# Gate and up projections of a feed-forward layer by seven block products instead of eight, and the split of the hidden values moved to the start of the down projection

## The chip, the cores and the metric

The kernel runs on 1 core of one Trainium2 chip. The metric is the device time in microseconds (us); smaller is better. TensorE multiplies, VectorE (DVE), ScalarE (ACT) and GpSimd (POOL) do elementwise work, SyncE (SP) issues the weight transfers.

## The reference, cut to what matters

Two transformer blocks over 512 tokens (528 with 16 meta tokens in front in part of the first block), d_model 1024, all in f32. Each block has two feed-forward layers (four in all) around a mixer:

```
h = h + 0.5 * rmsnorm(swiglu(rmsnorm(h, g), w_in, w_out), g2)      # block 1, twice; block 2 without the outer norm
swiglu(x) = (silu(x @ w_gate) * (x @ w_up)) @ w_down                # 1024 -> 2816 twice, 2816 -> 1024
```

D_FF is 2816, that is 22 tiles of 128 columns. The mixers between the feed-forward layers (an mLSTM, and a mixer of attention and retention) are not touched.

## The kernel before, in words

**Precision.** Every f32 operand of a large product is split in two f32r numbers, hi and lo = x - hi, and a product is three matmuls: hi*hi, hi*lo, lo*hi (`product`, L1467; its matmuls stand at L1472). ACT makes hi by a copy, DVE or POOL makes lo by a subtraction. Activations are kept transposed: 8 tiles of 128 features by 512 (or 528) tokens.

**Weights.** They come in units of 128 x 1024 (512 KB) through four slots: SP loads a unit into `raw`, ACT copies it to `whi` (`split_hi`, L454, L468), POOL subtracts into `wlo` (`pool_lo`, L367, L371), PE uses both. The semaphores count units: `raw_loaded`, `hi_done`, `lo_done`, `unit_done`. POOL serves the units strictly in order; ACT works three units ahead (AHEAD = 3). SP loads a unit when the lo of the unit four before is made.

**A feed-forward layer** (`pe_ffn` L1534, `act_ffn` L503, `dve_ffn` L919, `load_ffn` L311) has an up stage and a down stage. Up: for each of 22 tiles two units, gate and up, of 8 k-tiles each, so 48 matmuls of 512 columns (with 528 tokens: 96 of 264 columns, in two pieces). PE waits for `lo_done` of the unit and for the banks. DVE multiplies the gate sums by the norm factors `rbc` (L926), ACT applies silu (L509), DVE multiplies by the up sums (L931) and by rbc (L934), ACT makes hid_hi (L511) and DVE hid_lo (L936), all during the next tile's matmuls. Down: for each of 8 output tiles three units (8, 8 and 6 k-tiles) over the 22 hidden tiles. The first output tile waits, k by k, for `hid_ready`, and each output tile waits for `out_s["v_ready"]`, whose first two counts come from `free_out` (L944), three memsets that DVE issues ahead of `dve_ffn`.

**The norm.** The x operands xhi and xlo are made from hT times the gains before the norm factors are known; the first two tiles of PE's work run while the sum of squares is formed. `r_ready` on DVE waits for rbc, and then `dve_ffn` starts.

The order on each engine is written out by hand: each engine runs its own program in order, and only semaphores tie them together. ACT's and POOL's programs (`prog_scalar`, `prog_gpsimd` L429) call the parts in turn.

## Time and profile before

| what | us |
|---|---|
| median of 3 runs | 2214.21 (2208.22 to 2214.69) |
| the profiled execution's own time | 2211.47 |
| its span, first to last instruction | 2209.7 |
| TensorE busy | 2128.5 (96% of the span) |
| VectorE / ScalarE / GpSimd busy | 744.6 / 719.5 / 925.0 |
| mean granted TensorE clock | 0.98 of full speed |

How to read it: busy time is the union of an engine's instructions; weight loads (PEld) run beside matmuls. A matmul's own duration (some 0.40 us at 512 columns) holds its way through the array; what counts is the distance of one start to the next, which a row of many matmuls gives as its time divided by their number. In rows of the timeline the columns are start, duration, engine, line, operation, output <- inputs, count, and in brackets the idle time before and what ended it.

### The profile page before, as it was taken

The numbers are of one execution on the slowest core, as the hardware profiler recorded it, in microseconds if no ns is written. First come the engines' busy times: TensorE is split into PE (matmuls) and PEld (weight loads), VectorE is DVE, ScalarE is ACT, GpSimd is POOL, SyncE is SP. The second block draws the span as 40 slices with busy tenths as digits, with TensorE's granted clock in tenths as the row PEclk, the third lists the DMA queues.
The fourth block names the chain that finished last, engine by engine and source line by source line (L and its number), as shares of the span: only waits on it lengthen the run. The fifth ranks groups of instructions, "written<-read, shape, count | busy, mean of one in ns | idle before, by whom it ended". The sixth has DMA issues, their size and how long they took to land.

```text
span 2209.7 us, 28883 instructions
## 1 busy us (share of the span) xinstructions
PE 2128.5 (96%) x10959; PEld 1745.8 (79%) x10959; DVE 744.6 (34%) x1084; ACT 719.5 (33%) x993; POOL 925.0 (42%) x402
## 2 busy tenths in 40 slices
PE   8999999899999899999989999999989899999998
PEld 7999999887777688888868888886774377888887
DVE  5222210483374622220062222116657623222111
ACT  4222222333443422222242222224255424222222
POOL 3444344434453544445554444443333033444442
PEclk9999999999899999999999999999999999999999
DMA  5332233223202233323323333333211022333331
GB/s 148 96 95 86 83 94 91 57 65 86 72 1 67 65 97 95 95 88 89 99 67 95 95 95 88 93 96 89 74 39 29 1 67 85 95 95 95 89 95 55
DMA packets 333835, 176.98 MB, mean 80 GB/s; under 512 B 9539, under 2 KB 329278, under 8 KB 333774
## 3 DMA queue, kind: packets, MB, share of 16 engines
q1 hardware_dynamic: 331792, 175.07, 27.2%
q10 hardware_dynamic: 1982, 1.07, 0.2%
q8 instruction: 41, 0.67, 0.1%
q14 instruction: 20, 0.16, 0.0%
HBM read 174.02 MB, written 2.10 MB: 80 GB/s over the span
## 4 chain that ended last, share of the span: by engine, by line
PE 89%; DVE 7%; ACT 2%; issue 1%; DMA 0%; POOL 0%; SPq 0%; ACTq 0%; DVEq 0%; POOLq 0%
PE ps L1472 82%; PE ps L1948 1%; DVE wa L998 1%; DVE E L1023 1%; PE ps L1709 1%; PE ps L1500 1%; PE ps L1914 1%; DVE xlo L891 1%; PE ps L1705 1%; DVE small L1352 0%; DMA x_tok<-in_x 0%; PE ps L1740 0%; PE ps L1924 0%; DVE sinr L1160 0%; ACT PR L735 0%
## 5 line engine op out<-in xcount | busy, mean ns | idle before, releaser
L371 POOL TENSOR_TENSOR wlo<-raw,whi 128x1024 fp32r<-128x1024 f32 x336 | 829.6, 2471 | 1144.6 <-ACT whi L468 1144.4
L1472 PE MATMUL ps<-xhi,whi 128*128 128x512 f32 (+2 forms) x2224 | 728.2, 359 | 28.0 <-DVE xlo L891 17.7
L1472 PE MATMUL ps<-xlo,whi 128*128 128x512 f32 (+2 forms) x2224 | 720.7, 355 | 0.0
L1472 PE MATMUL ps<-xhi,wlo 128*128 128x512 f32 (+2 forms) x2224 | 719.2, 354 | 0.0
L468 ACT ACTIVATE whi<-raw 128x1024 fp32r<-128x1024 f32 x336 | 353.1, 1053 | 515.6 <-PE ps L1472 506.8
L1472 PEld LDWEIGHTS ps<-xhi,whi 128*128 128x128 f32 (+1 forms) x2224 | 392.3, 189 | 101.3 <-issue 21.3
L1472 PEld LDWEIGHTS ps<-xlo,whi 128*128 128x128 f32 (+1 forms) x2224 | 393.8, 190 | 63.6 <-issue 2.0
L1472 PEld LDWEIGHTS ps<-xhi,wlo 128*128 128x128 f32 (+1 forms) x2224 | 393.0, 189 | 61.5
L1472 PE MATMUL ps<-hid_hi,wlo 128*128 128x512 f32 (+1 forms) x880 | 280.5, 351 | 0.0
L1472 PE MATMUL ps<-hid_hi,whi 128*128 128x512 f32 (+1 forms) x880 | 279.5, 350 | 0.0
L1472 PE MATMUL ps<-hid_lo,whi 128*128 128x512 f32 (+1 forms) x880 | 278.9, 350 | 0.0
L511 ACT ACTIVATE hid_hi<-wb 128x512 f32 (+3 forms) x88 | 56.0, 637 | 462.7 <-DVE wb L934 462.7
L931 DVE TENSOR_TENSOR wb<-wa,ps 128x512 f32<-128x512 f32 (+1 forms) x88 | 60.9, 693 | 399.4 <-PE ps L1472 387.7
L1472 PEld LDWEIGHTS ps<-hid_lo,whi 128*128 128x128 f32 x880 | 153.8, 188 | 24.7
L1472 PEld LDWEIGHTS ps<-hid_hi,wlo 128*128 128x128 f32 x880 | 153.6, 188 | 23.5
L1472 PEld LDWEIGHTS ps<-hid_hi,whi 128*128 128x128 f32 x880 | 153.4, 188 | 22.9
L926 DVE TENSOR_TENSOR wa<-ps,rbc 128x512 f32<-128x512 f32 (+1 forms) x88 | 61.2, 695 | 223.3 <-PE ps L1472 206.5
L936 DVE TENSOR_TENSOR hid_lo<-wb,hid_hi 128x512 f32 (+1 forms) x88 | 65.2, 740 | 82.5 <-ACT hid_hi L511 82.5
L969 DVE SCALAR_TENSOR_TENSOR hT<-ps,hT 128x512 f32 x24 | 16.6, 692 | 224.3 <-PE ps L1472 224.3
L965 DVE TENSOR_SCALAR ybuf<-ps,vec 128x528 f32 (+1 forms) x16 | 12.2, 760 | 226.1 <-ACT sq L537 226.1
L934 DVE TENSOR_TENSOR wb<-wb,rbc 128x512 f32<-128x512 f32 (+1 forms) x88 | 62.1, 706 | 3.0
L509 ACT ACTIVATE wa<-wa 128x512 f32<-128x512 f32 (+1 forms) x88 | 54.4, 618 | 1.8 <-DVE wa L926 1.8
...
## 6 DMA issues: line engine op xcount, KB each, us to landing
...
```

The source lines that it names most:

```text
L371: pool.tensor_tensor(wlo[:, u % SLOTS, :], raw[:, u % SLOTS, :], whi[:, u % SLOTS, :].bitcast(F32), ALU.subtract).then_inc(lo_done, 1)
L468: act.activation(whi[:, s, :], raw[:, s, :], ACT.Copy).then_inc(hi_done, 1)
L509: act.activation(tile(wa, b, n), tile(wa, b, n), ACT.Silu).then_inc(s["silu_done"], 1)
L511: act.activation(tile(hid_hi, r * 2 + b, n), tile(wb, b, n), ACT.Copy).then_inc(s["hi_ready"], 1)
L891: v.scalar_tensor_tensor(out=tile(xlo, k, n), in0=tile(hT, k, n), scalar=gain(name, g0 + k), in1=tile(xhi, k, n).bitcast(F32), op0=ALU.mul ...
L926: v.tensor_tensor(tile(wa, b, n), bank(2 * b if n == TOK else b, n), tile(rbc, 0, n), ALU.mult) \
L931: v.tensor_tensor(tile(wb, b, n), tile(wa, b, n), bank(4 + 2 * b if n == TOK else 2 + b, n), ALU.mult) \
L934: v.tensor_tensor(tile(wb, b, n), tile(wb, b, n), tile(rbc, 0, n), ALU.mult).then_inc(s["product"], 1)
L936: v.tensor_tensor(tile(hid_lo, r * 2 + b, n), tile(wb, b, n), tile(hid_hi, r * 2 + b, n).bitcast(F32), ALU.subtract).then_inc(s["hid_ready ...
L998: v.tensor_tensor(tile(wa, k % 2, n), tile(value, k, n), tile(rbc, 0, n), ALU.mult).then_inc(s["t_ready"], 1)
L1023: link(v, "dve", v.scalar_tensor_tensor(out=cacc(b), in0=zpad(b)[:, j:j + TOK], scalar=w[j], in1=cacc(b), op0=ALU.mult, op1=ALU.add))
L1472: ins = pe.matmul(o, lhs[l], x[r], start=first and n == 0, stop=last and n == 2)
```

## The change

In each feed-forward layer 4 of the 22 up tiles (tiles 18 to 21, now first in time; called old tiles below) are made as before. The other 18 are made by Winograd's form of the 2x2 block product: the weights of a tile are four blocks of 512 columns (gate, k-tiles 0-3 = A11; gate, 4-7 = A12; up, 0-3 = A21; up, 4-7 = A22), x is cut in k halves and in token halves. Seven products of 4 k-tiles x 3 matmuls x half the tokens (256 or 264 columns) replace eight.

- Once per layer: DVE makes eight half tiles times gains and rbc twice over (`scaled`, 16 operations of 256 or 264 columns), four `differences` of 1024 (1056) columns; ACT makes seven hi operands of that width, DVE four lo, POOL three. They stand between the four old tiles.
- Per fast tile: ACT copies A21 to a PSUM bank, makes seven hi halves of 512, keeps three partial sums, and applies silu; DVE makes four weight sums, three lo, the corner, gate and hidden operations; POOL makes four lo. Multiplication by rbc after the matmuls is gone.
- The hidden tiles are stored in f32. Their split in hid_hi and hid_lo is made from the last fast tile on and in the first output tile of the down stage, in a new order of k (8..15, 18..21, 16, 17, 0..7). `free_out` is issued by DVE behind `dve_ffn`, ahead of its last ten splits.

The core of the diff (semaphore tables, tile addressing helpers and parts that repeat are left out):

```diff
+    def pool_ffn(pool, i):
+        f, s, n = FFNS[i], fast_s, FFNS[i]["n"]
+        u0 = f["u0"]
+        pool_lo(pool, u0 + AHEAD, u0 + 6)
+        pool.wait_ge(ffn_s["x_diff"], ffn_at[i]["x_diff"] + 4)
+        for q, name in enumerate(("A11", "A12", "S4")):
+            pool.wait_ge(ffn_s["x_hi"], ffn_at[i]["x_hi"] + q + 1)
+            pool.tensor_tensor(x_operand(xop, name, 1, n), x_operand(xop_f, name, 1, n),
+                               x_operand(xop, name, 0, n).bitcast(F32), ALU.subtract).then_inc(ffn_s["x_lo_pool"], 1)
+        pool_lo(pool, u0 + 6, u0 + 2 * NCONV)
...
+        def body(st):
+            r, c = st
+            nxt = (r, c + 1)
+            lo(st, "S3", operand(stage, i, "S3"), s["w_lo_pool"], 1)
+            more = r is not None or c + 1 < NFAST
+            if more:
+                lo(nxt, "A11", raw_blocks(i, c + 1)["A11"], s["w_lo_pool"], 1)
+                lo(st, "A22", raw_blocks(i, c)["A22"], s["w_lo_pool"], 1)
+                lo(nxt, "A12", raw_blocks(i, c + 1)["A12"], s["w_lo_pool"], 1)
+            else:
...
+        def hid_hi(first, last):
+            for at_ in range(first, last):
+                k = HID_ORDER[at_]
+                act.wait_ge(c_s["hid"], hid_made(i, k))
+                act.wait_ge(*freed_by(i, at_ ))
+                act.activation(hid_hi_tile(k, n), hid_tile(k, n), ACT.Copy).then_inc(c_s["hid_hi"], 1)
...
+        def body(st):
+            r, c = st
+            nxt = (r, c + 1)
+            first, last = r is None and c == 0, r is None and c == NFAST - 1
+            a, b, d = acc_banks(c)
...
+            keep(st, "M1", kept(n)[:, 0, :], a, free)
+            hi_sum(st, "S3", "M7")
+            if not last:
+                keep_a21(nxt)
+                hi_a11(nxt)
+            else:
+                hid_hi(0, 4)
+            keep(st, "M5", m5_of(n), d, None if first else done(i, "c22", before(st)))
+            if not last:
+                hi_sum(nxt, "S1", "M5")
+            else:
+                down_hi(0)
+            hi(st, "A22", raw_blocks(i, c)["A22"], "M4")
+            if last:
+                hid_hi(4, 7)
+            keep(st, "M6", kept(n)[:, 1, :], a, None)
+            if not last:
+                hi_sum(nxt, "S2", "M6")
+                hi(nxt, "A12", raw_blocks(i, c + 1)["A12"], "M2")
+            else:
+                hid_hi(7, 10)
+                down_hi(1)
+            act.wait_ge(*done(i, "gate", st))
+            act.activation(gates_of(n), gates_of(n), ACT.Silu).then_inc(s["silu"], 1)
+        split_to_conv(act, u0, 1)
+        silu(0)
+        split_to_conv(act, u0, 3)
+        x_hi(("A11", "A12", "S4"), c_s["x_ready"], c_at["x_ready"] + 1)
+        silu(1)
+        split_to_conv(act, u0, 5)
+        x_hi(("S1", "S3", "S2", "A22"), c_s["x_diff"], c_at["x_diff"])
+        silu(2)
...
+        if n == SEQ:
+            prepare()
+        silu(3)
+        if n == TOK:
...
+    def dve_ffn(v, i, rms, name, g0):
...
+        def conv(q):
+            b = q % 2
+            v.wait_ge(unit_done, STARTED + u0 + 2 * q + 1)
+            v.wait_ge(c_s["banks_free"], c_at["banks_free"] + q + 1)
+            v.tensor_tensor(tile(wa, b, n), bank(2 * b if n == TOK else b, n), tile(rbc, 0, n), ALU.mult) \
+             .then_inc(c_s["gate_scaled"], 1)
...
+            v.wait_ge(unit_done, STARTED + u0 + 2 * q + 2)
+            if q >= 2:
+                v.wait_ge(c_s["hid"], c_at["hid"] + q - 1)
+            v.tensor_tensor(tile(wb, b, n), tile(wa, b, n), bank(4 + 2 * b if n == TOK else 2 + b, n), ALU.mult) \
+             .then_inc(c_s["banks_free"], 1)
+            v.wait_ge(c_s["banks_free"], c_at["banks_free"] + q + 3)
+            v.tensor_tensor(tile(hid_f, NFAST + q, n), tile(wb, b, n), tile(rbc, 0, n), ALU.mult).then_inc(c_s["hid"], 1)
...
+        def scaled():
...
+            for g, ks in enumerate(((0, 1, 2, 3), (4, 5, 6, 7))):
+                for half in range(2):
+                    for k in ks:
+                        span = slice(o + half * h, o + (half + 1) * h)
...
+                    ins.then_inc(c_s["x_ready"], 1)
...
+        def differences():
+            part = lambda name: x_operand(xop_f, name, 1, n)
+            b12 = hid_f[:, B12_AT * TOK:B12_AT * TOK + 4 * h]
+            v.wait_ge(c_s["x_ready"], c_at["x_ready"] + 4)
+            v.tensor_tensor(part("S1"), b12, part("A11"), ALU.subtract).then_inc(c_s["x_diff"], 1)
+            v.tensor_tensor(part("S3"), part("S4"), b12, ALU.subtract).then_inc(c_s["x_diff"], 1)
+            v.wait_ge(c_s["x_diff"], c_at["x_diff"] + 1)
+            v.tensor_tensor(part("S2"), part("S4"), part("S1"), ALU.subtract).then_inc(c_s["x_diff"], 1)
+            v.wait_ge(c_s["x_diff"], c_at["x_diff"] + 3)
+            v.tensor_tensor(part("A22"), part("A12"), part("S2"), ALU.subtract).then_inc(c_s["x_diff"], 1)
+        def x_lo():
+            v.wait_ge(c_s["x_diff"], c_at["x_diff"] + 4)
+            for q, name in enumerate(("S1", "S3", "S2", "A22")):
+                v.wait_ge(c_s["x_hi"], c_at["x_hi"] + 4 + q)
+                v.tensor_tensor(x_operand(xop, name, 1, n), x_operand(xop_f, name, 1, n),
+                                x_operand(xop, name, 0, n).bitcast(F32), ALU.subtract).then_inc(c_s["x_lo_dve"], 1)
...
+        def corner(st):
+            a = acc_banks(st[1])[0]
+            v.wait_ge(*done(i, "M7", st))
+            v.wait_ge(*done(i, "m5_kept", st))
+            r, c = st
+            if not (r is None and c == 0):
+                v.wait_ge(c_s["hid"], count(c_at["hid"] + NCONV, st))
+            v.tensor_tensor(c22_of(n), ps[:, a, 0:h], m5_of(n), ALU.add).then_inc(s["c22"], 1)
...
+        def hidden(st):
+            r, c = st
+            a = acc_banks(c)[0]
+            if r is None and c == NFAST - 1:
+                v.wait_ge(unit_done, STARTED + u0 + NU_UP)
+            else:
+                v.wait_ge(*done(i, "M4", st))
+            v.wait_ge(*done(i, "silu", st))
+            v.wait_ge(*done(i, "c22", st))
+            v.tensor_tensor(hid_half(st, 0, n), ps[:, a, 0:h], gates_of(n)[:, 0, :], ALU.mult)
+            v.tensor_tensor(hid_half(st, 1, n), c22_of(n), gates_of(n)[:, 1, :], ALU.mult).then_inc(c_s["hid"], 1)
+        def hid_lo(first, last):
+            for at_ in range(first, last):
+                k = HID_ORDER[at_]
+                v.wait_ge(c_s["hid_hi"], c_at["hid_hi"] + at_ + 1)
+                if k < HID_IN_XLO:
+                    v.wait_ge(*freed_by(i, KF + k))
+                v.tensor_tensor(hid_lo_tile(k, n), hid_tile(k, n), hid_hi_tile(k, n).bitcast(F32), ALU.subtract) \
+                 .then_inc(c_s["hid_ready"], 1)
+        def body(st):
+            r, c = st
+            nxt, prev = (r, c + 1), (r, c - 1)
+            first, last = r is None and c == 0, r is None and c == NFAST - 1
+            if not first:
+                corner(prev)
+            lo(st, "S2")
+            s3(st)
+            lo(st, "S4")
+            if not last:
+                s1(nxt)
+                lo(nxt, "S1")
+            else:
+                hid_lo(0, 4)
+            if not first:
+                hidden(prev)
+            if not last:
+                s2(nxt)
+            else:
+                hid_lo(4, 8)
+            gate(st)
+            if not last:
+                s4(nxt)
+        conv(0)
+        scaled()
+        conv(1)
+        differences()
+        conv(2)
+        x_lo()
+        start = (None, 0)
+        if n == SEQ:
+            s1(start)
+            lo(start, "S1")
+            s2(start)
+        conv(3)
+        if n == TOK:
+            s1(start)
+            lo(start, "S1")
+            s2(start)
+        s4(start)
+        body(start)
+        with v.Fori(0, NFAST // 2 - 1) as r:
+            body((r, 1))
+            body((r, 2))
+        end = (None, NFAST - 1)
+        body(end)
+        corner(end)
+        hid_lo(8, 10)
+        hidden(end)
+        hid_lo(10, 12)
+        v.wait_ge(c_s["hid"], c_at["hid"] + KF)
+        def rest():
+            hid_lo(12, KF)
+        return rest
...
         free_out(v, 2, SEQ)
-        dve_ffn(v, 1, N2)
+        rest()
...
+        for q in range(2, NCONV):
+            for g in range(2):
+                unit(q // 2, q % 2, g)
+        pe_fast(pe, i)
...
                     pe.wait_ge(lo_done, r * 12 + (u + 1))
-                    for k in range(k0, k0 + kn):
+                    for k in piece:
                         if j == 0:
-                            pe.wait_ge(s["hid_ready"], at["hid_ready"] + k + 3)
-                        ins = product(pe, [o for o, _, _ in p], w_tile(u, k - k0),
...
+    def pe_fast(pe, i):
...
+        def multiply(name, bank_, start):
+            w = [operand(buf, i, name) for buf in (whi, wlo)]
+            x = [x_operand(xop, name, low, n) for low in range(2)]
+            for k in range(4):
+                for q, (l, r) in enumerate(((0, 0), (0, 1), (1, 0))):
+                    ins = pe.matmul(ps[:, bank_, 0:h], w[l][:, k * P:(k + 1) * P], x[r][:, k * h:(k + 1) * h],
+                                    start=start and k == 0 and q == 0, stop=k == 3 and q == 2, skip_group_check=True)
+            return ins
...
+        def body(st):
+            r, c = st
+            a, b, d = acc_banks(c)
+            first = r is None and c == 0
+            pe.wait_ge(*done(i, "lo_A11", st))
+            if first:
+                pe.wait_ge(c_s["banks_free"], c_at["banks_free"] + NCONV + 1)
+                pe.wait_ge(c_s["x_lo_pool"], c_at["x_lo_pool"] + 1)
+            elif r is None:
...
+            pe.wait_ge(*done(i, "lo_S1", st))
+            if first:
+                pe.wait_ge(c_s["gate_scaled"], c_at["gate_scaled"] + NCONV)
+                pe.wait_ge(c_s["x_lo_dve"], c_at["x_lo_dve"] + 4)
+                pe.wait_ge(c_s["x_lo_pool"], c_at["x_lo_pool"] + 3)
+            multiply("S1", d, True).then_inc(s["mult"], 2 if first else 1)
+            if not first:
+                m4((r, c - 1))
+            pe.wait_ge(*done(i, "lo_S2", st))
+            pe.wait_ge(*done(i, "m1_kept", st))
+            multiply("S2", a, False).then_inc(s["mult"], 1)
+            pe.wait_ge(*done(i, "lo_A12", st))
+            multiply("A12", b, True).then_inc(s["mult"], 1)
+            pe.wait_ge(*done(i, "lo_S4", st))
+            pe.wait_ge(*done(i, "m5_kept", st))
+            multiply("S4", d, False).then_inc(s["mult"], 1)
+            pe.wait_ge(*done(i, "lo_S3", st))
+            pe.wait_ge(*done(i, "u2_kept", st))
+            multiply("S3", a, False).then_inc(s["mult"], 1)
+        body((None, 0))
+        with pe.Fori(0, NFAST // 2 - 1) as r:
+            body((r, 1))
+            body((r, 2))
+        end = (None, NFAST - 1)
+        body(end)
+        m4(end)
```

## Rows read from the trace of the kernel before

**Rows 1.** The page: engines' busy time, and the chain that ended last by engine.
```profile
PE 2128.5 (96%) x10959; PEld 1745.8 (79%) x10959; DVE 744.6 (34%) x1084; ACT 719.5 (33%) x993; POOL 925.0 (42%) x402
...
PE 89%; DVE 7%; ACT 2%; issue 1%; DMA 0%; POOL 0%; SPq 0%; ACTq 0%; DVEq 0%; POOLq 0%
```

**Rows 2.** The chain in order of time, pieces of matmuls: start us, us, what.
```profile
39.78 370.07 PE ps L1472 x3042
...
1134.23 1.78 PE ps L1500 x16
...
1138.64 355.53 PE ps L1472 x1530
```

**Rows 3.** Windows of 512-column and of 264-column matmuls: stretch, us, busy by engine, clock.
```profile
59.50:71.20 11.70, 11.70 (x98) 11.70 (x98) 2.83 (x4) 3.20 (x4) 4.79 (x2) 1.00 0.32 93
1863.00:1874.15 11.15, 11.15 (x50) 9.02 (x49) 2.77 (x4) 3.17 (x4) 4.82 (x2) 1.00 0.32 94
```

**Rows 4.** Groups on VectorE: name, shapes, count | busy us, mean ns | idle.
```profile
L1088 DVE SCALAR_TENSOR_TENSOR E<-ps,E 128x512 f32<-128x512 f32 x8 | 5.5, 692 | 0.4
...
L1088 DVE SCALAR_TENSOR_TENSOR E<-ps,E 128x256 f32<-128x256 f32 x8 | 3.4, 425 | 0.3
```

**Rows 5.** Groups on ScalarE: copies of 1024 and 512, activations of 256.
```profile
L468 ACT ACTIVATE whi<-raw 128x1024 fp32r<-128x1024 f32 x336 | 353.1, 1053 | 515.6 <-PE ps L1472 506.8 <-DMA raw<-in_ffn_w_in 5.6 <-issue 3.1
...
L511 ACT ACTIVATE hid_hi<-wb 128x512 f32 x60 | 38.0, 633 | 330.7 <-DVE wb L934 330.7
...
L601 ACT ACTIVATE E<-ps,acol 128x256 f32<-128x256 f32 x8 | 3.6, 450 | 0.0
```

**Rows 6.** Groups on GpSimd: subtractions of 1024 and of 512.
```profile
L371 POOL TENSOR_TENSOR wlo<-raw,whi 128x1024 fp32r<-128x1024 f32 x336 | 829.6, 2471 | 1144.6 <-ACT whi L468 1144.4 <-POOL qT L426 0.2
...
L394 POOL TENSOR_TENSOR E_r<-E,Shi 128x512 fp32r<-128x512 f32 x8 | 10.2, 1277 | 0.3 <-ACT Shi L609 0.3
```

**Rows 7.** Timeline of VectorE where the third feed-forward layer begins: memset, tiles 0 and 2.
```profile
1137.12 0.48 DVE L947 MEMSET acc<- 128x512 f32 x1
...
1139.60 0.69 DVE L926 TENSOR_TENSOR wa<-ps,rbc 128x512 f32<-128x512 f32 x1 [1.98 <-ACT rbc L489]
...
1143.09 0.69 DVE L934 TENSOR_TENSOR wb<-wb,rbc 128x512 f32<-128x512 f32 x1
...
1154.71 0.69 DVE L931 TENSOR_TENSOR wb<-wa,ps 128x512 f32<-128x512 f32 x1 [2.81 <-PE ps L1472]
```

**Rows 8.** Timeline of VectorE in the fourth layer: eight operations in a row, tiles 0 and 2.
```profile
1824.49 5.39 DVE L891 SCALAR_TENSOR_TENSOR xlo<-hT,vec,xhi 128x512 fp32r<-128x512 f32 x8 [1.40 <-ACT xhi L498]
...
1840.84 0.69 DVE L926 TENSOR_TENSOR wa<-ps,rbc 128x512 f32<-128x512 f32 x1 [8.25 <-ACT rbc L489]
...
1861.52 0.69 DVE L931 TENSOR_TENSOR wb<-wa,ps 128x512 f32<-128x512 f32 x1 [4.78 <-PE ps L1472]
```

**Rows 9.** Timeline of VectorE in the first layer: tile 0 and tile 2.
```profile
40.82 0.71 DVE L926 TENSOR_TENSOR wa<-ps,rbc 128x528 f32<-128x528 f32 x1 [4.68 <-ACT rbc L491]
...
59.53 0.70 DVE L931 TENSOR_TENSOR wb<-wa,ps 128x528 f32<-128x528 f32 x1 [5.03 <-PE ps L1472]
```

**Rows 10.** Timeline of VectorE and GpSimd in the residual step, both reading SBUF twice.
```profile
1113.37 1.77 DVE L998 TENSOR_TENSOR wa<-ybuf,rbc 128x512 f32<-128x512 f32 x1
...
1115.07 0.74 DVE L891 SCALAR_TENSOR_TENSOR xlo<-hT,vec,xhi 128x512 fp32r<-128x512 f32 x1
1115.22 1.73 POOL L386 TENSOR_TENSOR hT<-hT,wa 128x512 f32<-128x512 f32 x1 [0.63 <-DVE wa L998]
...
1115.73 1.77 DVE L998 TENSOR_TENSOR wa<-ybuf,rbc 128x512 f32<-128x512 f32 x1
```

**Rows 11.** Windows around an idle TensorE: stretch, us, busy by engine, granted clock.
```profile
1522.00:1526.00 4.00, 0.42 (x2) 0.24 (x2) 3.74 (x11) 2.00 (x3) 0.00 (x0) 1.00 0.50 131
1526.00:1530.00 4.00, 4.00 (x10) 2.65 (x9) 0.28 (x1) 3.94 (x5) 2.37 (x1) 0.61 0.10 10
1530.00:1534.00 4.00, 4.00 (x18) 3.23 (x17) 0.00 (x0) 3.94 (x5) 0.00 (x0) 0.97 0.36 121
```

More of the change, by code:

```diff
@@ L135, in program @@
     whi = sb("whi", [P, SLOTS, UNIT], F32R)
+    with ExitStack() as r:
+        stage = r.enter_context(nc.sbuf_tensor("stage", [P, SLOTS, UNIT], F32))
     wlo = sb("wlo", [P, SLOTS, UNIT], F32R)
@@ L516, in act_ffn, with silu @@
-        with act.Fori(1, KF // 2) as r:
-            for b in range(2):
-                for e in (2 * b + AHEAD, 2 * b + AHEAD + 1):
-                    split_hi(act, u0 + e, r, 4)
-                gated(r, b)
-        cursor[0] += NU_UP - 4
+        f, s, n = FFNS[i], fast_s, FFNS[i]["n"]
+        c_s, c_at, u0 = ffn_s, ffn_at[i], f["u0"]
+        h = half_of(n)
+        def silu(q):
+            b = q % 2
+            act.wait_ge(c_s["gate_scaled"], c_at["gate_scaled"] + q + 1)
+            act.activation(tile(wa, b, n), tile(wa, b, n), ACT.Silu).then_inc(c_s["silu_done"], 1)
@@ new lines, in hi_a11, with hi_sum, keep @@
+        def hi_a11(st):
+            loaded(st, 0)
+            hi(st, "A11", raw_blocks(i, st[1])["A11"], "M1")
+        def hi_sum(st, name, product):
+            act.wait_ge(*done(i, name, st))
+            hi(st, name, ps[:, 7, :] if name == "S1" else operand(stage, i, name), product)
+        def keep(st, product, dst, bank_, free):
+            act.wait_ge(*done(i, product, st))
+            if free is not None:
+                act.wait_ge(*free)
+            act.activation(dst, ps[:, bank_, 0:h], ACT.Copy).then_inc(s["kept"], 1)
@@ L846, in e_tile, with half_of, count, done @@
         return (m1["E"] if buf is None else buf)[0:META if j == 0 else P, o:o + (EW[j] if w is None else w)]
+    MULTS = ["A11", "S1", "S2", "A12", "S4", "S3", "A22"]
+    def half_of(n):
+        return n // 2
+    def count(at, s):
+        r, c = s
+        return at + c if r is None else r * 2 + (at + c)
+    def done(i, name, st):
+        (r, c), (sem, at) = st, FAST_AT[name]
+        step = FAST[sem]
+        value = fast_at[i][sem] + step * c + at
+        return fast_s[sem], value if r is None else r * (2 * step) + value
```

377 lines of the change are left out of this document (294 added, 83 removed).

## The prediction, made before the change was run

> **What bounds the kernel now.** The page says it at once: TensorE is busy 96% of the span, and 89% of the chain that ended last is its work [rows 1]. So matmuls left out give time back only as far as TensorE stays fed. The chain in order of time gives the price of a matmul by its width: 1530 of 512 columns in 355.53 us, 232.4 ns each; 3042 of nearly all 264 columns in 370.07 us, 121.7 ns each [rows 2]. The windows of two up stages show the same, with nothing idle on TensorE and the other engines under half busy: an up tile is 11.15 us at 512 columns (48 matmuls) and 11.7 us at 2 x 264 (96) [rows 3].
>
> **What the seven products remove.** A fast tile has 7 x 12 = 84 matmuls. With 528 tokens they are 264 wide: 84 x 121.7 ns = 10.22 us instead of 11.68, 1.46 less. With 512 tokens they are 256 wide, a width that no row has. Bounds: 111 ns, what a weight load and one column take in the 16 column sums (1.78 us) [rows 2], and 121.7 ns at 264. I take 118 (121.7 x 256 / 264), as 264 is the nearer: 9.91 us instead of 11.16, 1.24 less. 18 tiles: 26.3 us in the first layer, 22.3 in each of three others, **93.2 us** in all (at 111 ns 120, at 121.7 ns 77).
> The Trainium skill (TensorE: Matmul & The Clock Gate, section Back-to-back issue gap) gives a sustained 131 ns at 512 columns and 81 at 128, so narrow matmuls would be poor value and 84 of 256 would take longer than 48 of 512. By it the fast tile would lose; the rows at 264, at 0.52 of the cost of 512, contradict it, and the sum goes by them.
>
> **The fast tile in its steady state.** Durations: DVE 0.69 us at 512 and 0.43 at 256 [rows 4]; ACT 0.63 and 0.45, 1.05 at 1024 [rows 5]; POOL 1.28 at 512, 2.47 at 1024 [rows 6]. DVE: 8 x 0.69 + 3 x 0.43 = 6.8 us; ACT: 9 x 0.63 + 3 x 0.45 = 7.0; POOL: 4 x 1.28 = 5.1, all under 9.9. The longest loop through them is lo S2, S3 (DVE), hi S3, A21 (ACT), S1 (DVE), hi S1 (ACT), lo S1, hidden, S2, gate, S4 (DVE) and back: independent operations start 0.6 us apart at 512 (eight in 5.39 us) [rows 8], a change of engine costs some 0.15, together 7.8 us. VectorE and GpSimd shut each other out when both read two SBUF operands: 1.77 us instead of 0.69, 1.73 instead of 1.28, and the one that asked first goes first [rows 10]. In a fast tile hidden and lo S2 can each meet a POOL operation: at most 2 x 1.28, 10.3 us. With phases laid out against TensorE's seven 1.42 us slots lo S2 ends 2.0 us into a tile and is needed at 4.25. I take 0, with up to 0.3 us a tile, 20 in all, as upper end. Weight loads (same bytes) stay hidden: they are asked for over 5 us before their use.
>
> **The joint at the start.** Here TensorE runs out of work. POOL's program makes lo of weight units 3 to 5, then waits for all four differences of x, makes three x lo of 1024, and only then lo of unit 6, which TensorE needs for the fourth old tile. From R, when rbc is there and DVE scales tile 0 (1139.60 in the third layer): tile 0 takes to R+4.2 [rows 7]; lo of unit 5 on POOL holds DVE 2.4; 16 scalings at 0.40 (0.66 at 512 [rows 8] less the 0.27 between 512 and 256 [rows 4]) 6.4; tile 1 3.3 (three DVE operations, silu, two changes of engine); four differences of 1024 at 1.2 (0.69 plus 0.53) 4.8. That is R+21.2. Then POOL: four of 2.47, and in between DVE's two-SBUF operations (tile 2's last multiply 0.7, first x lo 1.2), 11.8: unit 6 is ready at **R+33**. TensorE has finished unit 5 at R+15.1 in the third layer [rows 7] and in the second, whose start repeats it; at R+20.7 in the fourth [rows 8]; at R+18.7 in the first [rows 9], where 264-wide work gives R+33.4. So it stands 17.9, 17.9, 12.3 and 14.7 us. After some 3.6 us idle the granted clock was 0.61 over the next 4 us [rows 11], about 2 us lost: 8 more. Later VectorE work ends 0.3 late at M6 (three layers); in the first layer the A21, A11 and S1 preparation comes behind tile 3: 3.4. Sum **75 us**. Lower bound, if DVE and POOL never met: R+28.6, in all 58.
>
> **The joint at the end.** Before, hidden tiles were split during the up tiles and the down stage began without a stall. Now twelve hid_lo, and lo of down units 0 and 1 (2.47 each), stand ahead of it. In the last body, counted from its M1 (M4 could end at 11.3): ACT puts four hid_hi, down unit 0 and three hid_hi ahead of keeping M6 (ends 9.2; M7 delayed 0.7). DVE: lo S4 to 3.2, four hid_lo with POOL's lo S3 between to 7.2, hidden with POOL's lo A22 to 9.0, then POOL's down unit 0 to 11.45, one hid_lo, POOL's down unit 1 to 14.5, three hid_lo, gate and corner to 17.3. Corner releases the last M4: 18.8. Then hidden, hid_lo 10 and 11 (waiting for hid_hi behind silu), and `free_out`'s two memsets of 0.48 [rows 7], whose count the down stage waits for: 22.0. That is 10.7 late; half clock adds 1.1 on M4 and 2.0 on the down stage [rows 11]: 13.8, four times **55 us**. Without any meeting of DVE and POOL the same list gives 16.1, 4.8 late, 19 in all. I take 13.8, since rows 10 show the meeting. The last ten hid_lo are then ahead of use (0.7 us each on TensorE). Nothing else moves: down matmuls are as many, transfers too; the multiplications by rbc that go were under cover.
>
> **Sum.** 2211.5 (the profiled execution's own time, 2.7 under the median) - 93.2 + 75 + 55 = **2248**.
>
> **Rivals.**
> - *DVE and POOL hardly meet* (faster). For: only two-SBUF operations exclude each other, and a few tenths move them apart. Then start 58, end 19: 2211.5 - 93.2 + 77 = 2195. It decides where the two joints cost less than 23.3 us a layer together. Against: POOL has some 20 us of work in the 33 us from R, DVE as much. Chance 0.22.
> - *Only the end is cheap* (same): hid_lo and down units miss each other, the start does not: -93.2 + 75 + 19, 2212. Chance 0.11.
> - *The fast loop is bound by VectorE's chain* on top of the joints: +20, 2268; DVE would be the releaser of M6 in every tile. Chance 0.11.
> - *Width does not pay*: 256 columns take 133 ns (11.15 / 84), so the three layers of 512 tokens save nothing: +67, 2315. For: weight loads fill the window of 264-wide matmuls (11.70 of 11.70) [rows 3], so something other than columns may bound there. Against: even so 264 columns took 121.7 ns. Chance 0.03. The Trainium skill's rule named above would make it so, or worse.
>
> **How the numbers follow.** Forecast 0.53 (its own range 2225 to 2268), rivals 0.22, 0.11, 0.11, 0.03. About 0.3% (6.6 us) is what a measurement can tell from no change. Slower 0.53 + 0.11 + 0.03 = 0.67; same 0.11; faster 0.22. The range reaches to 2196, the case of no meetings, and to 2272.
>
> **What would show it.** Right: per layer, PE idle 12 to 18 us before the fourth old tile, released by POOL wlo, whose last four operations follow x_diff; clock 0.5 to 0.6 behind it; fast tiles 9.9 us (10.2) apart; M4 of the last tile waiting for DVE's corner, and the first down matmul for DVE's memset, together about 14 us late. POOL's 2.47 us operations lengthen hid_lo to over 2 us. Wrong: unit 6's lo early, or the idle at both joints under 23 us a layer, or fast tiles over 10.3 us apart with M6 waiting for lo S2.

## The result and the profile after

The changed kernel takes **2250.22 us** (2247.83 to 2255.06, 4 runs) against 2213.06 (2208.22 to 2214.69, 4 runs) of the kernel before: ratio 1.0174, 95% interval 1.0151 to 1.0198. It is slower by 37 us, though 72 of its 88 up tiles pass one eighth fewer columns through TensorE. The forecast of 2248 stands, and so do its signs; what follows asks whether each step of it was the one that acted.

The page of the changed kernel, the rows that answer to [rows 1]:

```profile
PE 2065.7 (92%) x12687; PEld 1790.6 (80%) x12687; DVE 1271.2 (57%) x1752; ACT 999.8 (44%) x1669; POOL 1005.2 (45%) x558
...
PE 79%; DVE 12%; ACT 2%; issue 2%; POOL 2%; DMA 0%; SPq 0%; DVEq 0%; ACTq 0%; POOLq 0%
```

TensorE has 63 us less to do, but its share of the chain that ended last fell by ten points, and VectorE's rose from 7% to 12%: time left the matmuls and came back as waits for other engines. TensorE is idle for 182.3 us of the span (2248.0 - 2065.7), where it was for 81.2 (2209.7 - 2128.5).

The chain in order of time (start us, us, what), whose rows answer to [rows 2]. The x16 rows are column sums that stand just before and just after a feed-forward layer, and serve as marks; L2086 is the fast tiles, L1949 the old block products and the down stage (line numbers shift by a few in the experiments' kernels).

```profile
89.95 182.12 PE ps L2086 x1488
...
754.77 1.78 PE ps L1977 x16
...
809.57 168.09 PE ps L2086 x1416
997.68 125.75 PE ps L1949 x528
...
1124.20 1.99 PE ps L1977 x16
1153.04 1.78 PE ps L1977 x16
1206.78 163.82 PE ps L2086 x1380
1394.71 130.16 PE ps L1949 x549
1524.87 1.68 PE ps L1977 x16
```

Three things are to be read here. A matmul of 264 columns took 122.4 ns (182.12 / 1488) and one of 256 took 118.7 (168.09 / 1416, and 163.82 / 1380 again): forecast 121.7 and 118. Pieces of 1380 to 1488 of a layer's 1512 fast matmuls stand unbroken, so in the steady state nobody kept TensorE waiting. And between a layer's two marks lie 371.83 us in the third layer, where the same marks of the kernel before (1134.23 and 1494.18) are 359.95 apart. By such marks the time came from:

| stretch | before | after | difference | forecast |
|---|---|---|---|---|
| start to the end of the mixer before layer 2 | 748.98 | 754.77 | +5.8 | +7.6 |
| layer 2 | 356.92 | 369.43 | +12.5 | +11.7 |
| layer 3 | 359.95 | 371.83 | +11.9 | +11.7 |
| mixer before layer 4 | 329.81 | 331.58 | +1.8 | 0 |
| layer 4 | 373.83 | 378.42 | +4.6 | +6.1 |

The short stretches left out and the end add some 1.7. The forecast of a layer is its two joints less its 18 tiles, from the prediction's terms.

The waits of TensorE that the change brought (engine and tile, releaser: us in all, how many, the longest):

```profile
PE ps L1949 <- POOL wlo L405: 59.6, 4, 17.0
PE ps L2086 <- DVE sq L1322: 23.2, 4, 5.9
PE ps L1949 <- DVE cell L1421: 13.5, 4, 3.4
```

The first is the start joint, once in each of four layers; the next two are the end joint, the last M4 behind the corner and the first down matmul behind the memset of `free_out`. (M1 to M7 are a fast tile's seven products. TensorE makes them in the order M1, M5, then M4 of the tile before, M6, M2, M3, M7; M6 needs lo of the weight sum S2.) These three are 96.3 us of standing.

**The start joint.** VectorE in the third layer (start, us, line, tiles, [idle before]), the rows that answer to [rows 7], and GpSimd beside it:

```profile
1158.12 0.69 DVE L1230 TENSOR_TENSOR wa<-ps,rbc 128x512 f32<-128x512 f32 x1 [2.78 <-ACT rbc L567]
...
1181.62 13.24 DVE L1269 TENSOR_TENSOR xop<-xop_f,xop 128x1024 fp32r<-128x1024 f32 x4
```

```profile
1178.73 8.45 POOL L471 TENSOR_TENSOR xop<-xop_f,xop 128x1024 fp32r<-128x1024 f32 x3 [14.03 <-DVE xop_f L1262]
1187.15 6.63 POOL L405 TENSOR_TENSOR wlo<-raw,whi 128x1024 fp32r<-128x1024 f32 x2
```

R is 1158.12. GpSimd stands 14.03 us for the last difference of x (ready at R+20.6; forecast R+21.2), makes three x lo in 8.45, and then lo of unit 6, ready at R+32.4 (forecast R+33). Meanwhile VectorE's four x lo of 1024, 1.2 each when alone, take 13.24. Both engines are busy and each goes at the other's pace: while one has an operation with two SBUF inputs running, such an operation of the other has to wait (x lo of 1.2 us comes to 3.3 here). Below this is called the lock. TensorE starts the fast tiles at 1203.42 and M6 of the first at R+48.7.

**The end joint** in the third layer, VectorE and then TensorE:

```profile
1379.52 7.86 DVE L1353 TENSOR_TENSOR hid_r<-hid_f,xop 128x512 fp32r<-128x512 f32 x4
...
1387.91 0.41 DVE L1322 TENSOR_TENSOR sq<-ps,sq 128x256 f32<-128x256 f32 x1
...
1394.39 0.06 DVE L1421 MEMSET cell<- 128x1 f32 x1
```

```profile
1388.46 0.77 PE L2086 MATMUL ps<-xop,whi 128*128 128x256 f32 x2 [5.87 <-DVE sq L1322]
1394.71 0.77 PE L1949 MATMUL ps<-xop,whi 128*128 128x512 f32 x1 [3.35 <-DVE cell L1421]
```

Four hid_lo, 0.69 each when alone, take 7.86 while GpSimd makes lo of the two first down units (1380.65, 5.58 us for both). Gate and corner stand behind them, M4 behind the corner, the down stage behind hidden, hid_lo and the memsets: it starts 22.7 us after the last tile's M1 (about 1372.0). Forecast: 22.0, and 1.1 for the clock.

**The clock** in windows of both joints (stretch, us, PE, PEld, DVE, ACT and POOL busy, granted clock, DMA share, GB/s), answering to [rows 11]:

```profile
1178.00:1182.00 4.00, 0.00 (x0) 0.00 (x0) 2.92 (x5) 3.10 (x5) 3.27 (x2) 0.50 0.01 2
1190.00:1194.00 4.00, 3.48 (x8) 2.81 (x9) 4.00 (x2) 0.00 (x0) 4.00 (x3) 0.50 0.44 131
1194.00:1198.00 4.00, 4.00 (x18) 3.20 (x18) 2.76 (x4) 1.09 (x2) 2.02 (x1) 0.98 0.45 131
...
1388.00:1392.00 4.00, 2.90 (x12) 2.64 (x12) 2.12 (x5) 2.19 (x4) 0.00 (x0) 0.50 0.32 98
1392.00:1396.00 4.00, 1.29 (x3) 1.14 (x4) 3.89 (x7) 3.81 (x7) 2.16 (x1) 0.50 0.00 0
1396.00:1400.00 4.00, 4.00 (x13) 3.13 (x13) 4.00 (x6) 2.87 (x5) 1.27 (x2) 0.63 0.46 131
```

After each of these waits TensorE works at the lower level (0.50, 1.2 GHz) for its next 4 us or so: 8 matmuls of 512 columns in 1190 to 1194, 18 in the next 4 us.

### The profile page after: what moved, and what is told of

The parts are those of the page before. It is cut to its first block, busy times and chain, and to the rows that moved or that the text cites. A ratio compares the mean times of both kernels' runs of the same rounds, so it can differ in the third digit from the quotient of the medians.

```text
span 2248.0 us, 35362 instructions
## 1 busy us (share of the span) xinstructions
PE 2065.7 (92%) x12687; PEld 1790.6 (80%) x12687; DVE 1271.2 (57%) x1752; ACT 999.8 (44%) x1669; POOL 1005.2 (45%) x558
## 4 chain that ended last, share of the span: by engine, by line
PE 79%; DVE 12%; ACT 2%; issue 2%; POOL 2%; DMA 0%; SPq 0%; DVEq 0%; ACTq 0%; POOLq 0%
PE ps L1949 41%; PE ps L2086 31%; POOL xop L471 2%; DVE hid_r L1353 1%; PE ps L2496 1%; DVE wa L1471 1%; DVE xop_f L1247 1%; DVE E L1496 1%; PE ps L2257 1%; PE ps L1977 1%; PE ps L2462 1%; DVE xlo L1191 1%; PE ps L2253 1%; POOL wlo L405 1%; DMA raw<-in_ffn_w_in 0%
## 5 line engine op out<-in xcount | busy, mean ns | idle before, releaser
L405 POOL TENSOR_TENSOR wlo<-raw,whi 128x1024 fp32r<-128x1024 f32 x192 | 491.6, 2564 | 665.8 <-ACT whi L546 634.9
L2086 PE MATMUL ps<-xop,whi 128*128 128x256 f32 (+1 forms) x4032 | 728.3, 283 | 29.4 <-DVE sq L1322 23.2
L2086 PEld LDWEIGHTS ps<-xop,whi 128*128 128x128 f32 x4032 | 626.1, 190 | 31.6 <-issue 26.1
L2086 PE MATMUL ps<-xop,wlo 128*128 128x256 f32 (+1 forms) x2016 | 571.4, 283 | 0.0
L2086 PEld LDWEIGHTS ps<-xop,wlo 128*128 128x128 f32 x2016 | 381.3, 189 | 0.0
L477 POOL TENSOR_TENSOR wlo<-raw,whi 128x512 fp32r<-128x512 f32 x212 | 287.9, 1363 | 164.0 <-ACT whi L619 164.0
L1949 PE MATMUL ps<-xhi,whi 128*128 128x512 f32 (+3 forms) x784 | 273.6, 378 | 88.7 <-POOL wlo L405 59.6
L1949 PE MATMUL ps<-xop,whi 128*128 128x512 f32 (+1 forms) x1120 | 328.4, 354 | 13.5 <-DVE cell L1421 13.5
L1949 PE MATMUL ps<-xop,wlo 128*128 128x512 f32 (+1 forms) x880 | 283.2, 354 | 0.0
L1949 PE MATMUL ps<-xlo,whi 128*128 128x512 f32 (+3 forms) x784 | 265.0, 367 | 0.0
L1949 PE MATMUL ps<-xhi,wlo 128*128 128x512 f32 (+3 forms) x784 | 263.8, 365 | 0.0
L1949 PEld LDWEIGHTS ps<-xhi,whi 128*128 128x128 f32 (+2 forms) x784 | 142.8, 194 | 125.3 <-POOL wlo L405 61.1
L1949 PEld LDWEIGHTS ps<-xop,whi 128*128 128x128 f32 x1120 | 194.5, 190 | 45.5 <-issue 14.5
L619 ACT ACTIVATE whi<-stage 128x512 fp32r<-128x512 f32 x216 | 136.6, 633 | 211.5 <-DVE stage L1293 121.7
L1949 PE MATMUL ps<-hid_r,whi 128*128 128x512 f32 (+1 forms) x640 | 206.5, 356 | 0.0
L1949 PEld LDWEIGHTS ps<-xop,wlo 128*128 128x128 f32 x880 | 155.6, 190 | 23.9
L1949 PEld LDWEIGHTS ps<-xlo,whi 128*128 128x128 f32 (+2 forms) x784 | 143.4, 194 | 24.9 <-issue 2.0
L1949 PEld LDWEIGHTS ps<-xhi,wlo 128*128 128x128 f32 (+2 forms) x784 | 142.5, 193 | 24.4
```

The costliest lines, as they stand in the source:

```text
L405: pool.tensor_tensor(wlo[:, u % SLOTS, :], raw[:, u % SLOTS, :], whi[:, u % SLOTS, :].bitcast(F32), ALU.subtract).then_inc(lo_done, 1)
L477: pool.tensor_tensor(operand(wlo, i, name), source, operand(whi, i, name).bitcast(F32), ALU.subtract) \
L619: ins = act.activation(operand(whi, i, name), source, ACT.Copy)
L1949: ins = pe.matmul(o, lhs[l], x[r], start=first and n == 0, stop=last and n == 2)
L2086: ins = pe.matmul(ps[:, bank_, 0:h], w[l][:, k * P:(k + 1) * P], x[r][:, k * h:(k + 1) * h], start=start and k == 0 and q == 0, stop=k == ...
```

## The experiments

All times are medians; the kernel before gave 2213.1 beside the change, 2211.1 beside the runs called a, 2212.5 beside b and c, 2210.3 beside d, so differences of medians between these groups are good to some 3 us. An edit is to the changed kernel, with its 2250.2, where nothing else is said. Waits, spans and busy times are those of one profiled execution of each kernel, so they are compared with each other and not with medians.

### a1_pool_order: the start joint, GpSimd's order

```
-        pool_lo(pool, u0 + AHEAD, u0 + 6)
+        pool_lo(pool, u0 + AHEAD, u0 + 2 * NCONV)
         pool.wait_ge(ffn_s["x_diff"], ffn_at[i]["x_diff"] + 4)
...
-        pool_lo(pool, u0 + 6, u0 + 2 * NCONV)
```

> GpSimd makes lo of weight units 6 and 7 before its three x operands; nothing else moves. Theory (the start joint is GpSimd's order: unit 6's lo stands behind the differences and the x operands): TensorE goes straight from unit 5 to unit 7, the idle time of 17, 17, 12 and 14 us before unit 6 goes, and a shorter one comes back at the first fast tile, where the x operands are late (M5 about 38 us after rbc is there instead of 47): 7 to 10 us less in each layer, 2212 to 2222 in all against 2250. Rival (the vector work between rbc and the first fast tile sets the start by itself, whatever the order): the idle time only moves from unit 6 to the first fast tile, 2245 to 2250.

Measured: 2237.77 (2233.39 to 2238.14), ratio 1.0112 [1.0095, 1.0129]: 12.5 less than the change, 3.1 a layer, between the two expectations and in neither. The wait of 17.0 us for unit 6 is gone (one of 1.98 us for the bank is left in the third layer), and others stand in its place; first TensorE's, then VectorE in the third layer:

```profile
PE ps L2085 <- POOL wlo L476: 27.4, 4, 11.6
```

```profile
1167.89 3.43 DVE L1256 TENSOR_TENSOR xop_f<-hid_f,xop_f 128x1024 f32<-128x1024 f32 x1
...
1177.84 10.00 DVE L1268 TENSOR_TENSOR xop<-xop_f,xop 128x1024 fp32r<-128x1024 f32 x4
...
1190.36 0.68 DVE L1229 TENSOR_TENSOR wa<-ps,rbc 128x512 f32<-128x512 f32 x1
...
1194.30 0.69 DVE L1310 TENSOR_TENSOR wlo<-stage,whi 128x512 fp32r<-128x512 f32 x1
```

The lo of unit 6 that was moved ahead now meets a difference of x instead (3.43 us instead of 1.21). R is 1149.98 here, so VectorE reaches lo of S2, which the first tile's M6 needs, at R+44.3; in the change it did so at R+47.7 (1205.80). TensorE stands 6.89 us before M1 for GpSimd's weight lo, 2.54 before M5 for the L1229 row above (M5 starts at R+41.2, expected R+38), 1.23 before M6, and starts M6 at R+45.3 instead of R+48.7. There is a **second wall** right behind the first: what VectorE does one after the other from R (differences, x lo, S1, S2, the last old tile, S4). Taking GpSimd's order away exposes it. The clock takes a part too: over the whole kernel TensorE's idle time falls by 22.9 us (182.3 to 159.4), but its busy time for the same 12687 matmuls rises by 11.2 (2065.7 to 2076.9), while several short waits follow each other with the clock at 0.50 (third layer, two of three such windows in a row):

```profile
1186.00:1190.00 4.00, 2.61 (x12) 2.31 (x11) 3.29 (x5) 0.60 (x1) 0.00 (x0) 0.50 0.00 0
...
1194.00:1198.00 4.00, 2.77 (x14) 2.75 (x14) 2.79 (x5) 3.27 (x7) 1.66 (x2) 0.50 0.25 70
```

### a2_banks_early, a3_pool_waits, a4_corner_first: the end joint

a2 lets the down stage have its banks before `free_out`; the same two increments, each moved to where its bank has been read:

```
+        v.memset(cell[:, 2:3], 0.0).then_inc(out_s["v_ready"], 1)
         corner(end)
         hid_lo(8, 10)
         hidden(end)
+        v.memset(cell[:, 1:2], 0.0).then_inc(out_s["v_ready"], 1)
```

> VectorE gives the banks to the down stage by one small memset after the last gate and one after the last hidden tile, instead of behind the memsets of free_out. Theory (the first down matmul waits for free_out, not for data): the first down matmul follows the last M4 at once, some 3 us earlier in each layer, and the splits that it then meets are made: 2236 to 2241 against 2250. Rival (the first down stage is bound by the splits of the hidden tiles): the 3 us come back as waits for hid_lo within the first output tile, 2247 to 2250.

Measured: 2243.18 (2240.82 to 2243.88), 1.0140 [1.0123, 1.0157]: 7.0 less, between the two expectations: each is half right. The 13.5 us behind the memset are gone; 9.7 us of shorter waits for hid_lo come in.

a3 adds a wait to GpSimd and nothing else: lo of the down units only when the last tile's corner has been read.

```
         body((None, NFAST - 1))
+        pool.wait_ge(*done(i, "c22", (None, NFAST - 1)))
         return u0 + NU_UP
```

> A wait is added: GpSimd makes lo of the first down units only when VectorE has made the corner of the last fast tile. Theory (GpSimd's two operations of 2.4 us shut VectorE's splits out ahead of gate and corner): the last M4 starts about 5 us earlier after M7 (idle about 1 us instead of 6), the first down matmul 3 to 5 us earlier in each layer, 2230 to 2240 against 2250, although a wait was added. Rival (VectorE simply has too many splits ahead of the corner): M4 starts as late as before, and the down stage a little later for the late lo of its unit: 2250 to 2256.

Measured: 2237.17 (2234.68 to 2240.48), 1.0121 [1.0104, 1.0138]: 13.0 less, as the theory had it. TensorE's waits:

```profile
PE ps L2087 <- DVE sq L1323: 5.9, 4, 1.6
PE ps L1950 <- DVE cell L1422: 26.5, 4, 6.7
```

M4's wait shrinks from 23.2 to 5.9 us in all with not one VectorE operation less: GpSimd beside it was its cause. 13.0 of these 17.3 us come back at the next wait (13.5 in the change, 26.5 here), since hid_lo and the memsets behind the corner now meet what GpSimd put off. So only 4.3 us of waits went, but 15.2 us of span (2248.0 to 2232.8). The rest is clock: TensorE's busy time for the same 12687 matmuls fell by 11.2 us (2065.7 to 2054.5). In the third layer M4 (from 1373.76) falls into the first of these windows, at full clock, where the change had 0.50 for M4 and for the start of the down stage (windows above).

```profile
1372.00:1376.00 4.00, 1.90 (x15) 1.52 (x13) 4.00 (x6) 3.13 (x5) 2.15 (x1) 1.00 0.38 110
...
1380.00:1384.00 4.00, 1.97 (x5) 1.61 (x6) 3.89 (x6) 4.00 (x8) 2.37 (x1) 0.50 0.46 131
```

a4 gives gate and corner precedence and makes every hid_lo of the last eight behind them:

```
             else:
-                hid_lo(0, 4)
...
             else:
-                hid_lo(4, 8)
             gate(st)
...
         corner(end)
-        hid_lo(8, 10)
+        hid_lo(0, 2)
         hidden(end)
-        hid_lo(10, 12)
+        hid_lo(2, 12)
```

> VectorE makes gate and corner of the last fast tile before any split of a hidden tile. Theory: M4 follows M7 within 1 us (5 to 6 us earlier), but the count for the banks stands behind all twelve splits in free_out, so that the first down matmul starts no earlier, rather 0 to 3 us later in each layer: 2250 to 2262. Rival (the order ahead of the corner is what the end joint costs): the down stage starts 5 us earlier in each layer, 2228 to 2232.

Measured: 2268.07 (2263.08 to 2271.57), 1.0248 [1.0231, 1.0266]: **18 more**, and 6 above the range of the theory, which had the first down matmul 0 to 3 us later in each layer.

```profile
PE ps L1945 <- DVE cell L1417: 55.9, 4, 14.1
```

M4 starts nearly at once (1.8 us of waits in all), and the first down matmul stands 14.1 us, because the memset that frees its banks stands behind ten hid_lo. So hid_lo ahead of the corner was not the fault by itself.

b1_corner_banks puts a2's and a4's edits together, so that neither the corner nor the banks wait for hid_lo.

> Four old tiles as in the change, gate and corner ahead of the splits and the banks given early. Theory as for c3: the first output tile of the down stage ends no more than 2 us earlier than in the changed kernel: 2240 to 2250. Rival: 2200 to 2215.

Measured: 2239.21 (2235.79 to 2240.74), 1.0119 [1.0094, 1.0144]: 11.0 less than the change, 29 less than a4, at the lower edge of the theory and far from the rival. The down stage now waits 21 times, at most 1.8 us, 25.2 us in all, for the split itself. Its twelve hid_lo are work that has to be done somewhere beside GpSimd's, and 7 to 13 us of the end joint's 55 is what a2, a3 and this pair give.

### c1_six, c2, c3: six old tiles instead of four

The second wall stands 44 to 48 us behind R. TensorE has finished the third old tile at R+15.1 (third layer, from the prediction) and has one more of 11.2 us, so it is covered to R+26. Two more old tiles cover it to R+49. Their price is two tiles' gain a layer, 2 x 1.40 us in the first and 2 x 1.19 in the others, 9.9 us in all. c1 has 16 fast tiles (ScalarE's matching steps and the addressing of the hidden tiles are left out below):

```
-NCONV = 4
+NCONV = 6
...
-    FFN_PIECES = [[8, 9, 10, 11, 12, 13, 14, 15], [18, 19, 20, 21, 16, 17], [0, 1, 2, 3, 4, 5, 6, 7]]
+    OLD = [18, 19, 20, 21, 16, 17]
+    FFN_PIECES = [OLD, [8, 9, 10, 11, 12, 13, 14, 15], [0, 1, 2, 3, 4, 5, 6, 7]]
...
-        pool_lo(pool, u0 + AHEAD, u0 + 6)
+        pool_lo(pool, u0 + AHEAD, u0 + 10)
...
         x_lo()
+        conv(3)
+        conv(4)
...
-        conv(3)
+        conv(5)
```

> Six old tiles instead of four (16 fast ones), GpSimd's lo of weight units up to 9 ahead of its x operands. Theory (the start joint is the 40 to 45 us that VectorE, with GpSimd in its way, needs from rbc to the first fast tile, against 26 us of matmuls in the old tiles): two more old tiles give TensorE 22 us more work, the idle time between rbc and the fast loop goes to under 2 us a layer; eight fast tiles less cost 10, the idle time and the half clock give back 60 to 70 (75 forecast): 2180 to 2200 against 2250, under the 2211 of before. Rival (the idle time comes from the order of the work, moved with it): still 10 us or more idle in each layer, 2240 to 2260.

Measured: 2230.89 (2229.53 to 2233.04), 1.0085 [1.0061, 1.0108]: 19.3 less than the change, but far from the 2180 to 2200 of the theory, which had allowed under 2 us of idle time a layer there; the longest single wait is also under the rival's 10, and neither range holds. TensorE's waits, and VectorE in the third layer (R is 1150.61):

```profile
PE ps L1955 <- DVE wb L1240: 26.6, 9, 4.7
```

```profile
1168.53 3.41 DVE L1261 TENSOR_TENSOR xop_f<-hid_f,xop_f 128x1024 f32<-128x1024 f32 x1
...
1182.88 13.45 DVE L1273 TENSOR_TENSOR xop<-xop_f,xop 128x1024 fp32r<-128x1024 f32 x4
1196.25 0.68 DVE L1234 TENSOR_TENSOR wa<-ps,rbc 128x512 f32<-128x512 f32 x1
```

The wait for operands has turned into a wait for **banks**: an old tile's two banks come free when VectorE multiplies it out, and that stood behind 13.45 us of x lo.

c2_six_end adds a2's and a3's edits to c1, c3_six_corner adds a2's and a4's.

> The same with the banks given early (as in a2) and GpSimd's wait for the corner (as in a3). Theory (the two joints are independent, and at the end a2 and a3 measured 7 and 13 us): another 15 to 22 us less than c1, 2160 to 2185. Rival (the two cures of the end meet at the same wait): no better than a3's 13 alone.

> Six old tiles, gate and corner ahead of the splits (as in a4) and the banks given early: the last M4 follows M7, the first down matmul follows M4, and the first output tile then waits for each hid_lo in turn. Theory (the splits of 22 hidden tiles, 14 us on VectorE and as much on ScalarE, with GpSimd's 2.4 us between them, are what the end joint costs, in whatever order): 5 to 15 us less than c1, no better than c2. Rival (the wait of M4 for the corner and of the down stage for the banks are the cost): 35 to 50 us less than c1.

Measured: c2 2220.49 (2217.65 to 2224.67), 1.0038 [1.0026, 1.0051]; c3 2222.25 (2221.08 to 2226.18), 1.0048 [1.0033, 1.0063]. They are 10.4 and 8.6 under c1. c3 is as its theory had it (5 to 15, no better than c2), and it can be compared with b1, the same edits with four old tiles, which gave 11.0: so far the two joints are nearly independent. c2's range (2160 to 2185) missed as c1's did, and so did its difference, 15 to 22 us under c1: 10.4 is no more than a3's 13.0 alone, which was the rival. In its trace the wait behind the memset is gone, but 15.9 us of waits for hid_lo and 4.3 for GpSimd's lo of the first down unit have come in: the two cures of the end meet at the same work and do not add up. They were not run together with four old tiles.

### d1_six_banks: VectorE's order

One line of c1 is moved:

```
+        conv(3)
         x_lo()
-        conv(3)
         conv(4)
```

> c1_six with one thing more: VectorE splits unit 3 to 5's outputs of the third convolution step before it makes the lo halves of x, so that the banks of the old tiles come free earlier. What VectorE does serially at the start joint sets when the seventh block product can begin: with this theory the first fast tile starts some 6 to 7 us earlier in each layer than in c1_six (2230.9), and the time is 2200 to 2215. Rival: the total of VectorE's work up to its last lo half is unchanged and that total sets the start: 2225 to 2231.

Measured: **2202.78** (2202.47 to 2206.97), 0.9967 [0.9952, 0.9982]: 28.1 less than c1, 7.0 a layer, as the theory had it. In the third layer the first fast tile starts at R+54.2 instead of R+61.3.

```profile
PE ps L1955 <- DVE wb L1240: 8.5, 5, 2.1
```

```profile
1171.22 0.69 DVE L1240 TENSOR_TENSOR wb<-wa,ps 128x512 f32<-128x512 f32 x1 [0.70 <-ACT wa L590]
...
1172.67 11.25 DVE L1273 TENSOR_TENSOR xop<-xop_f,xop 128x1024 fp32r<-128x1024 f32 x4
```

Tile 3's banks are free at 1171.9, before the x lo. VectorE does the same work in the same lock with GpSimd; only what TensorE waits for stands earlier. Of 26.6 us of waits for banks 8.5 are left. Between the two profiled executions the span fell by 24.0 us (2229.1 to 2205.1): 13.9 of it is idle time of TensorE (147.9 to 134.0), as some other waits came out longer, and 10.1 is busy time for the same 12495 matmuls (2081.2 to 2071.1), that is clock. It agrees with what c1's longest wait (4.7 us), which is gone here, cost behind it; c1's windows around it:

```profile
1194.00:1198.00 4.00, 0.00 (x0) 0.00 (x0) 3.30 (x3) 0.63 (x1) 1.25 (x1) 0.82 0.61 181
1198.00:1202.00 4.00, 3.54 (x8) 2.84 (x9) 3.23 (x6) 1.67 (x3) 0.58 (x1) 0.50 0.11 32
1202.00:1206.00 4.00, 4.00 (x16) 3.22 (x15) 1.65 (x3) 1.75 (x3) 1.19 (x2) 0.82 0.00 0
```

0.50 of 3.54 us and 0.18 of 4.00 are 2.5 us; four layers of that are the 10.1.

### d2_six_dve and d4_four_dve: who makes x lo

Both take the three x lo from GpSimd and give them to VectorE, d2 in d1, d4 in the change.

```
         pool.wait_ge(ffn_s["x_diff"], ffn_at[i]["x_diff"] + 4)
-        for q, name in enumerate(("A11", "A12", "S4")):
-            pool.wait_ge(ffn_s["x_hi"], ffn_at[i]["x_hi"] + q + 1)
-            pool.tensor_tensor(x_operand(xop, name, 1, n), ...
             v.wait_ge(c_s["x_diff"], c_at["x_diff"] + 4)
+            for q, name in enumerate(("A11", "A12", "S4")):
+                v.wait_ge(c_s["x_hi"], c_at["x_hi"] + q + 1)
+                v.tensor_tensor(x_operand(xop, name, 1, n), ...
```

> d1_six_banks, and VectorE makes all seven lo halves of x, GpSimd none. If the lock that the two engines share is the cost, a GpSimd operation of 2.4 us that shuts VectorE out is replaced by one of 1.14 us on VectorE: some 3 us a layer less than d1, 2188 to 2202. Rival, VectorE's own load is the cost: 3 more operations of 1.14 us in each of 4 layers, 14 us more than d1.

> The changed kernel with four old tiles, and VectorE making all seven lo halves of x, so that unit 6's lo half on GpSimd waits for none of them. Theory (the lock is the cost): 3 to 4 us a layer less than a1_pool_order (2237.8), so 2222 to 2230. Rival (VectorE's serial work is the cost, whoever locks it out): 2238 to 2252.

Measured: d2 2203.67 (2202.13 to 2209.03), 0.9970 [0.9960, 0.9981], no different from d1; d4 2235.71 (2232.89 to 2239.49), 1.0110 [1.0089, 1.0132], no different from a1 (1.0112). Neither theory is right for either. VectorE in the third layer of d4:

```profile
1176.42 4.59 DVE L1264 TENSOR_TENSOR xop<-xop_f,xop 128x1024 fp32r<-128x1024 f32 x3
1180.93 4.62 DVE L1268 TENSOR_TENSOR xop<-xop_f,xop 128x1024 fp32r<-128x1024 f32 x4
...
1188.07 0.68 DVE L1225 TENSOR_TENSOR wa<-ps,rbc 128x512 f32<-128x512 f32 x1
```

Seven x lo on VectorE take 9.2 us where four beside GpSimd's three took 10.00 in a1. An x lo that GpSimd makes costs VectorE (10.00 - 4.62) / 3 = 1.8 us of standing in the lock; one that it makes itself costs 1.5. **Sharing the work between them gives next to nothing**, neither way. What TensorE waits for in d4 is the last old tile's bank (8.3 us for the L1225 row at 1188.07, R+39.5), the same wall as in a1 under another name: M6 starts at R+44.4, in a1 at R+45.3.

### d3_six_dve_end: all together

d2 with a2's and a3's edits.

> d2_six_dve with both edits of the end joint (banks released ahead of the split, GpSimd's lo halves held until the last fast tile has been combined). c2 against c1 gave 10.4 for these two; if the joints are independent, the same here: 2180 to 2192, below the kernel before (2212) by more than 1%. Rival: an earlier start joint leaves the end unchanged but GpSimd late there: within 3 us of d2.

Measured: **2196.40** (2191.44 to 2198.02), 0.9925 [0.9905, 0.9945]: faster than both kernels, by 0.5 to 0.95% than the one before, though 4 us outside the range that was expected. The end's two edits gave 7.3 instead of 10. The windows of its third layer, first the start joint, then the end:

```profile
1150.00:1154.00 4.00, 4.00 (x13) 3.12 (x13) 4.00 (x2) 1.32 (x2) 4.00 (x2) 0.66 0.41 114
...
1162.00:1166.00 4.00, 3.38 (x15) 2.77 (x16) 3.23 (x6) 2.28 (x3) 3.22 (x2) 1.00 0.01 4
```

```profile
1362.00:1366.00 4.00, 2.01 (x6) 1.32 (x6) 4.00 (x3) 0.00 (x0) 4.00 (x2) 0.79 0.51 150
1366.00:1370.00 4.00, 2.89 (x7) 1.82 (x6) 3.47 (x4) 0.00 (x0) 1.11 (x1) 0.50 0.70 206
```

At the start TensorE stands 2.06 us and 1.35 us for banks, and only the first costs it clock (0.66). At the end it stands longer, and at 0.50: VectorE's hid_lo and GpSimd's lo of the down units still meet (both busy all of 1362 to 1366), though no run parts them there. Sixteen fast tiles a layer without any joint would be 79.5 us under the kernel before (16 x 1.40 + 48 x 1.19); 14 are had. So even here the joints take some 65.

## Why the prediction was right, and where it was not

- **Gain of the seven products**, forecast 93.2: 84 matmuls took 10.28 us (at 122.4 ns) and 9.97 (at 118.7), so the gain is 18 x 1.40 + 54 x 1.19 = 89.5. The choice of 118 ns, from the nearer row, was off by 0.7. With it falls the rival that width does not pay, and for this kernel so do the sustained rates of the Trainium skill (TensorE: Matmul & The Clock Gate, section Back-to-back issue gap), 131 ns at 512 columns: these traces show 232.4 and 118.7 ns at 512 and 256.
- **Steady state at nothing**: confirmed by the unbroken pieces; no wait for lo of S2 is among TensorE's. The rival of a loop bound by VectorE falls.
- **Start joint, 75**: the four waits are 59.6 where 62.8 was forecast. Unit 6 was ready at R+32.4 for R+33. But the prediction tied the wait to POOL's order, and that is only half of the cause. a1 takes the order away and gets 12.5 us back, not 60, because VectorE's own list reaches lo of S2 at R+47.7 in the change and at R+44.3 in a1. The prediction had this in one clause, "0.3 late at M6": TensorE's M6 and VectorE's list come to the same place, so a second wall was to be read there. (M6 waited 0.35 us, by the trace for ScalarE's copy of M1; lo of S2 was ready 0.3 us before.) The expectation for a1 (2212 to 2222) did not take it from there, and the most obvious repair missed it by 16 us.
- **End joint, 55**: 22.7 us from the last M1 to the down stage, for 23.1. M4's wait is the lock's (a3: 23.2 to 5.9 us); the wait behind it is that for `free_out` (a2: its 13.5 us gone, 7.0 us of time).
- **Rivals of cheap joints** (2195 and 2212): refuted. VectorE and GpSimd meet in every joint of every layer: 13.24 us for four x lo of 1.2, 7.86 for four hid_lo of 0.69. That d3 comes to 2196, the time of one of them, is a coincidence: it has two fast tiles fewer and still pays for its joints.
- **Sum**: against the profiled execution's 2211.5, 89.5 gained and 127.8 lost give its 2249.85; forecast 93.2 and 130. That it is so near is in part luck. By the prediction's terms 109.9 of the loss was idle time (62.8, 4 x 10.7, and 0.9 and 3.4 for the later work) and 20.4 clock (8 and 4 x 3.1). TensorE's idle time rose by 101.1 (81.2 to 182.3), so 26.7 are left for the clock: the one was forecast 9 too high, the other 6 too low, and the gain 4 too high. The first layer came out 2.9 less than by its term (31.0 for 33.9, its fast tiles' gain added back to +5.8), layer 4 came out 2.4 less; why was not asked. The start of the kernel is unchanged: the first column sums stand at 32.14, before at 32.36. The 1.8 us in the mixer before layer 4 is no effect of the change: the same stretch took from 328.6 to 333.0 us in the traces of the experiments, none of which touches it.
- **Slips in the working**: at 111 ns the gain would be 124, not 120. Eight operations in 5.39 us [rows 8] start 0.67 us apart and not 0.6, which makes the longest loop some 0.5 us longer than 7.8. Neither changes the forecast.
